# Two query tiles of a head pair as one attention step, with the late scores inside a projection half unit

## What is computed

```
qa, ka = rms_norm over each head;  qr, kr = rope(...)        # rotary on the retention queries and keys
# prompt: query chunk c (64 frames) attends to its own chunk and the 8 before it, so to all keys <= its chunk
logits = q @ k^T * 64**-0.5 + bias[head, clipped distance];  p = softmax(logits);  o = p @ v
# sample: 64 queries attend to 512 cached keys and their own 64
```

## The kernel before

| short name | on PE | what follows elsewhere |
|---|---|---|
| S | `scores(k)`, L1951; sample tile L1958 to L1960 | DVE `add_bias` (L1260), ACT `exponentials` (L759, L763), DVE `scale_probs` (L1269, L1273) |
| H | `half_unit`, L1901 | DVE rotation, then the low part of the next unit |
| P | `probs(k-1)`: transposes, L1973, L1976 | ACT `probs_out`, copies to `pt` (L744, L746) |
| V | `values(k-2)`: p times v, L1993, L1998 | ACT `attn_out` once per pair |
| C | `cache_keys`: transposes of cached keys, L1938 | ACT copies to `kc_t` (L726); the sample tile's scores need it |

## Time and profile before

### The profile page before, as it was taken

How to read it: one execution, slowest core, us unless ns; L and a number is a source line. 1 busy time by engine, 2 the same in 40 slices (tenths; PEclk the granted TensorE clock), 3 DMA queues, 4 the chain that set the end, 5 groups by cost and what they waited for, 6 DMA issues and landing times.

```text
span 1425.9 us, 29063 instructions
## 1 busy us (share of the span) xinstructions
PE 1417.3 (99%) x10910; PEld 1376.4 (97%) x10910; DVE 1002.2 (70%) x1946; ACT 623.2 (44%) x1097; POOL 46.9 (3%) x89
## 2 busy tenths in 40 slices
PE   9999999999999999999999999999999999999999
PEld 8998889999999999999999988899999999999998
DVE  7348755879998359995442777567899963799832
ACT  5223445746554125553222245456465531355421
POOL 2001100100000000000010011001000000000000
PEclk9999999999999999999999999999999999999999
DMA  8223421332333223323253253115133332333332
GB/s 243 80 66 116 130 60 49 124 103 77 101 88 110 83 74 91 102 79 102 70 148 89 60 159 93 46 53 164 54 103 94 88 102 61 95 109 92 94 92 74
DMA packets 226511, 136.22 MB, mean 96 GB/s; under 512 B 4777, under 2 KB 220513, under 8 KB 226417
## 3 DMA queue, kind: packets, MB, share of 16 engines
q1 hardware_dynamic: 220240, 113.82, 28.5%
q0 software_dynamic: 5936, 20.82, 4.6%
q10 hardware_dynamic: 240, 0.32, 0.1%
HBM read 122.04 MB, written 8.18 MB: 91 GB/s over the span
## 4 chain that ended last, share of the span: by engine, by line
PE 96%; DVE 3%; issue 1%; ACT 1%; DVEq 0%; ACTq 0%
PE ps L1753 37%; PE ps L2164 34%; PE ps L1901 13%; PE ps L1951 2%; PE ps L1993 1%; PE ps L1973 1%; PE ps L1803 1%; PE ps L2244 1%; DVE sc L1260 1%; PE ps L2044 0%; DVE lo_of L1053 0%; PE ps L1811 0%; PE ps L2053 0%; PE ps L2071 0%; PE ps L1998 0%
## 5 line engine op out<-in xcount | busy, mean ns | idle before, releaser
L1753 PE MATMUL ps<-act,hi_down 128*128 128x288 f32 x1364 | 271.9, 295 | 0.0
L1753 PE MATMUL ps<-mix,hi_of 128*128 128x288 f32 x1216 | 243.7, 296 | 1.1 <-DVE lo_of L1053 1.0
L1753 PEld LDWEIGHTS ps<-act,hi_down 128*128 128x128 f32 x1364 | 218.4, 188 | 0.0
L1901 PE MATMUL ps<-mix,hi_of 128*128 128x288 f32 x1024 | 211.3, 300 | 0.0
L1753 PE MATMUL ps<-act,lo_down 128*128 128x288 f32 x682 | 201.0, 295 | 0.0
L1753 PEld LDWEIGHTS ps<-mix,hi_of 128*128 128x128 f32 x1216 | 194.3, 188 | 2.0 <-DVE lo_of L1053 1.5
L1753 PE MATMUL ps<-mix,lo_of 128*128 128x288 f32 x608 | 179.1, 295 | 0.0
L1901 PEld LDWEIGHTS ps<-mix,hi_of 128*128 128x128 f32 x1024 | 162.6, 188 | 10.4 <-issue 8.0
L1901 PE MATMUL ps<-mix,lo_of 128*128 128x288 f32 x512 | 150.8, 295 | 0.0
L901 ACT ACTIVATE hi_S<-sum_S 128x512 fp32r<-128x512 f32 x176 | 106.5, 628 | 95.3 <-DVE sum_S L1477 93.7
L2164 PE MATMUL ps<-sums_a,hi_A 128*128 128x288 f32 x704 | 142.7, 295 | 0.2
(11 more groups left out here) (272 smaller groups left out, 2698.0 us busy)
## 6 DMA issues: line engine op xcount, KB each, us to landing
raw_of<-in_w_in SPq DMA_DIRECT2D x56, 512.0 KB, 3.8
raw_down<-in_w_down SPq DMA_DIRECT2D x32, 704.0 KB, 4.6
pair_raw<-in_w_gate SPq DMA_DIRECT2D x42, 512.0 KB, 4.0
pair_raw<-in_w_up SPq DMA_DIRECT2D x42, 512.0 KB, 5.2
raw_of<-in_w_out SPq DMA_DIRECT2D x16, 512.0 KB, 4.1
mix<-att POOLq DMA_DIRECT2D x8, 576.0 KB, 5.8
strip_even<-bias_lines POOLq DMA_DIRECT2D x8, 320.0 KB, 5.9
strip_odd<-bias_lines POOLq DMA_DIRECT2D x8, 320.0 KB, 5.5
```

The source lines that it names most:

```text
L1753: last = nc.tensor.matmul(ps[:, bank + half, 0:HALF], weights(w, slot, nk)[:, k, :], tile[:, part, HALF * half:HALF * half + HALF], start= ...
L1901: last = nc.tensor.matmul(ps[:, half_bank(i), 0:HALF], weights(w, n % 2, KD)[:, k, :], mix[:, k, part, HALF * half:HALF * half + HALF], st ...
```

## The change

Tiles 0 and 1 of a pair become one item. Its scores lie side by side in a PSUM bank (128 and 256 columns), it has one round of waits, six transposes in one P, and the value products of both tiles in one V. A layer has 16 items instead of 20, and 18 steps, each with a half unit. The sample tile's scores are issued within their step's half unit, after 18 of its 24 matmuls. In that step DVE does the rotation ahead of `add_bias`. The small tiles `least`, `sums` and `rsum` are widened from 2 to 4 columns. The rotations of the six early half units use another scratch row (`qk_masked_row`), so that the first of them waits for `qk_lo` instead of `tok_ps`; the wait on `tok_ps` now stands ahead of the attention loop. Counts of semaphores follow the number of items.

```diff
@@
         PAIRS = HA // 2
-        ITEMS_A = [(p, t) for p in range(PAIRS) for t in range(TT)]
+        TILES_A = ((0, 1), (2,), (3,), (QT,))
+        IA = len(TILES_A)
+        ITEMS_A = [(p, tiles) for p in range(PAIRS) for tiles in TILES_A]
         NA = len(ITEMS_A)
         STEPS_A = NA + 2
...
-        AT_A = [k for k in range(STEPS_A) if k % TT != QT - 1]
+        AT_A = list(range(STEPS_A))
...
+        def keys_of(tiles):
+            at = [sum(P * (u + 1) for u in tiles[0:i]) for i in range(len(tiles) + 1)]
+            return [(t, slice(at[i], at[i + 1])) for i, t in enumerate(tiles)]
@@ ScalarE
                 for k in range(STEPS_A):
-                    if k >= TT + 2 and (k - 2) % TT == 0:
-                        attn_out((k - 2) // TT - 1)
-                    if k % TT == 3 and k < NA:
-                        cache_keys(k // TT)
+                    if k >= IA + 2 and (k - 2) % IA == 0:
+                        attn_out((k - 2) // IA - 1)
+                    if k % IA == IA - 1 and k < NA:
+                        cache_keys(k // IA)
@@ VectorE, half_unit
+                        swapped = qk_masked_row if i < PRE else vt[:, 0, :]
                         nc.vector.tensor_tensor(dst, bank, rcos[:, c], ALU.mult)
-                        nc.vector.tensor_tensor(vt[0:H, 0, c], bank[H:P, :], rsin[H:P, c], ALU.mult)
...
+                        nc.vector.tensor_tensor(swapped[0:H, c], bank[H:P, :], rsin[H:P, c], ALU.mult)
...
                     if i == 0:
-                        dve.wait_ge(tok_ps, 3 * TT * l + TT)
+                        dve.wait_ge(qk_lo, l + 1)
                     half_unit(i)
@@ VectorE, the loop of the attention steps
+                dve.wait_ge(ret_ready, 16 * l + PRE)
+                dve.wait_ge(tok_ps, 3 * TT * l + TT)
                 for k in range(STEPS_A + 1):
-                    if k < NA:
+                    late = k < NA and k % IA == IA - 1
+                    if k < NA and not late:
                         add_bias(k)
                     if k - 1 in AT_A:
                         half_unit(PRE + AT_A.index(k - 1))
-                    if k % TT == 1 and k < NA:
-                        decode_queries(k // TT)
+                    if late:
+                        add_bias(k)
+                    if k % IA == 1 and k < NA:
+                        decode_queries(k // IA)
                     if k < NA:
                         scale_probs(k)
@@ TensorE
-                def half_unit(i):
+                def half_unit(i, before_last=None):
...
                     for k in range(KD):
+                        if before_last and k == KD - 2:
+                            before_last()
                         for j, (w, part) in enumerate(PASSES):
...
-                        for hh in range(2):
-                            hr = head_rows(hh)
-                            last = nc.tensor.matmul(ps[:, 2 + hh, 0:P * (t + 1)], q_rev[hr, p, tok(t)], keys[hr, 0:P * (t + 1)],
-                                                    start=True, stop=True)
+                        for t, some in keys_of(tiles):
+                            for hh in range(2):
+                                hr = head_rows(hh)
+                                last = nc.tensor.matmul(ps[:, 2 + hh, some], q_rev[hr, p, tok(t)], keys[hr, 0:P * (t + 1)],
+                                                        start=True, stop=True)
...
                 for k in range(STEPS_A):
-                    late = k % TT == QT
+                    late = k % IA == IA - 1
                     if k < NA and not late:
                         scores(k)
                     if k in AT_A:
-                        half_unit(PRE + AT_A.index(k))
-                    if k < NA and late:
-                        scores(k)
+                        half_unit(PRE + AT_A.index(k), (lambda: scores(k)) if k < NA and late else None)
...
-                    if k % TT == 2 and k < NA:
-                        cache_keys(k // TT)
+                    if k % IA == 2 and k < NA:
+                        cache_keys(k // IA)
```

More of the change, by code:

```diff
@@ L735, in probs_out @@
                 def probs_out(k):
-                    p, t = ITEMS_A[k]
+                    p, tiles = ITEMS_A[k]
                     eng.wait_ge(pt_ps, NA * l + k + 1)
@@ L755, in exponentials @@
                         eng.wait_ge(sums_inv, NA * l + k - 1)
-                    if t < QT:
-                        for hh in range(2):
-                            e = sc[:, k % 2, hh, 0:P * (t + 1)]
-                            last = nc.scalar.activation(e, e, ACT.Exp, scale=-1.0, bias=least[:, k % 2, hh:hh + 1],
-                                                        accum_out=sums[:, k % 2, hh:hh + 1])
+                    if tiles[0] < QT:
+                        for i, (t, some) in enumerate(keys_of(tiles)):
+                            for hh in range(2):
+                                e, c = sc[:, k % 2, hh, some], 2 * i + hh
+                                last = nc.scalar.activation(e, e, ACT.Exp, scale=-1.0, bias=least[:, k % 2, c:c + 1],
+                                                            accum_out=sums[:, k % 2, c:c + 1])
                     else:
@@ L1248, in add_bias @@
                     strip = strips[p % 2]
-                    for hh in range(2):
+                    for i, hh in [(i, hh) for i in range(len(tiles)) for hh in range(2)]:
+                        t, some = keys_of(tiles)[i]
                         if t < QT:
                             r, w = slice(0, P), P * (t + 1)
-                            src, bias, dst = ps[:, 2 + hh, 0:w], strip[:, hh, STRIP - w:STRIP], sc[:, k % 2, hh, 0:w]
-                            c = hh
+                            src, bias, dst = ps[:, 2 + hh, some], strip[:, hh, STRIP - w:STRIP], sc[:, k % 2, hh, some]
+                            c = 2 * i + hh
                         else:
@@ L1264, in scale_probs @@
                 def scale_probs(k):
-                    p, t = ITEMS_A[k]
-                    n = 2 if t < QT else 1
+                    p, tiles = ITEMS_A[k]
+                    n = 2 * len(tiles) if tiles[0] < QT else 1
                     dve.wait_ge(exped, NA * l + k + 1)
@@ L1270, in scale_probs @@
                     dve.wait_ge(sums_inv, NA * l + k + 1)
-                    for hh in range(n):
-                        e = sc[:, k % 2, hh, 0:P * (t + 1)] if t < QT else sc_dec[:, k % 2, 0:TOK]
-                        last = nc.vector.tensor_scalar(e, e, rsum[:, k % 2, hh:hh + 1], None, ALU.mult)
+                    for c in range(n):
+                        t, some = keys_of(tiles)[c // 2]
+                        e = sc[:, k % 2, c % 2, some] if t < QT else sc_dec[:, k % 2, 0:TOK]
+                        last = nc.vector.tensor_scalar(e, e, rsum[:, k % 2, c:c + 1], None, ALU.mult)
                     last.then_inc(p_scaled, 1)
@@ L1933, in cache_keys @@
                     if p:
[L1935 removed]
+                        pe.wait_ge(s_ps, NA * l + IA * p)
                         pe.wait_ge(ot_out, PAIRS * l + p)
@@ L1969, in probs @@
                     wait_apart(pe, *waits)
-                    if t < QT:
+                    if tiles[0] < QT:
                         for hh in range(2):
-                            for s in range(t + 1):
+                            for s in range(keys_of(tiles)[-1][1].stop // P):
                                 last = nc.tensor.transpose(ps[:, 4 + hh, P * s:P * s + P], sc[:, k % 2, hh, P * s:P * s + P], ident)
```

52 lines of the change are left out of this document (27 added, 25 removed).

## The result

The changed kernel takes 1422.88 us (median of 8 runs, 1422.09 to 1423.36), the kernel before 1427.19 us beside it (1426.74 to 1427.76). The ratio is 0.9968, with a 95% interval of 0.9958 to 0.9977. That is 4.3 us faster, where 7.7 were predicted, and 0.5 us above the range. The profiled execution took 1423.22 us, its span is 1421.4 us against 1425.9.

What follows compares the result with a forecast made beforehand. PE's own instruction stream, busy for 99% of the span, was taken as the bound. 0.82 for each of 8 pairs (6.6) and 6 x 0.21 (1.3) made 7.8, taken as 7.7: 1419.4 us, range 1417.3 to 1422.4.

Steps and rivals of the forecast that it cites:

- rival A: Merged scores on PE: second tile's weights cannot load while the first streams; 1.7 us less gain, 1421.1; chance 0.12.
- rival B: DVE later than reckoned, so PE's wait before the next pair's first scores stays; 1.3 us less gain; chance alone 0.06.
- rival C: ACT's `kc_t` copy late, PE stands still inside a half unit; 1435 at 3.2 late; 0.05 in part, 0.03 slower, shared.
- Part 7: Early rotations on DVE: the first can start some 2 us earlier; worth 0, bounds 0 and 2 x 0.55.
- rival D: Rotation ahead of the bias delays DVE beyond 1.7 room; 8 us per us beyond 2.3; 0.05 in part, 0.03 slower, shared.
- five parts: PE's priced gains per pair: scores, transposes, values, cached keys, together 0.82, and the wait before the next scores, 0.21.
- 1 scores of tiles 0 and 1: PE, per pair: both tiles' scores in one group take 0.84 instead of 1.05; gain 0.21.
- 2 six transposes together: PE, per pair: six transposes at 0.80, as measured on tile 2, instead of 1.10; gain taken as 0.28.
- 3 values of tiles 0 and 1: PE, per pair: both tiles' values in one group of 12 loads take 0.80 instead of 0.96; gain 0.16.
- 4 cached keys: PE, per pair: cached keys' transposes, now followed by a half unit of the same shape, take 0.42 for 0.59; gain 0.17.
- 5 wait before the next scores: PE: sample scores start 0.79 earlier, so the wait before the next pair's scores loses 0.21, six times, 1.3 us.
- its other bound: Six transposes on PE reckoned from 0.44 for two plus 2 x 0.11 x 2, giving 0.88 instead of 0.80.

Runs made afterwards that it cites:

- sixth experiment: The changed kernel with the cached keys' transposes between the values of tile 0 and tile 1, two more shape changes per pair: 1425.52 us.
- first experiment: The changed kernel with ACT's copy of token tile 0 between the exponentials of tiles 0 and 1 in each layer's first attention step: 1421.47 us.
- seventh experiment: The changed kernel with the cached keys' transposes between the half unit and the six transposes, no longer behind the values: 1422.99 us.

## Why the prediction was right and where it failed

The mechanism was right and the sum too large, by 3.4 us: 7.7 predicted, 4.3 measured between the medians.

**Right.** The merged scores take 0.85 (0.84 predicted), so rival A is out. By the rule of the Trainium skill (TensorE: Matmul & The Clock Gate, Part 3: Packing small matmuls) the second tile's loads, in the same row groups, would not have overlapped and the group would take 1.05; the trace shows eight loads within 0.52 and 0.85 in all, so the rule did not decide here. The prediction said that no scores before could show it, but they did: of tile 0's four loads in two halves of rows the third starts at 145.66, while the first two matmuls run and 0.1 before the next one starts at 145.76. The merged values took 0.80 as predicted, the cached keys gained 0.20 instead of 0.17, and a change of shape costs 0.17 by the sixth experiment. The wait for `least` went (rival B out). ACT ended `kc_t` at 188.54, 1.22 ahead of the sample scores at 189.76, where 1.2 was worked out (rival C out). DVE's low part was ready at 189.31, 2.0 before the sample scores' bias at 191.31, where 1.7 was worked out. That bias ended at 192.86, 0.69 before the scores at 193.55, where 0.6 was. The rows, in the third pair:

```profile
187.95 0.59 ACT L733 ACTIVATE kc_t<-ps 128x512 f32<-128x512 f32 x1
```

```profile
188.08 1.23 DVE L1061 TENSOR_TENSOR lo_of<-raw_of,hi_of 128x1024 fp32r<-128x1024 f32 x1 [1.14 <-ACT hi_of L641]
...
191.31 0.75 DVE L1270 CUSTOM_DVE_ANT_0 sc<-ps,strip_even 64x576 f32<-64x576 f32 x1 [2.01 <-PE ps L1979]
...
192.78 0.08 DVE L1270 DVE_READ_ACCUMULATOR2_ANT least<- 64x1 f32 x1
```

Part 7 was priced at 0 and is 0. The wait of the earlier trace rows is still there:

```profile
113.43 0.19 PEld L1930 LDWEIGHTS ps<-qk_part,spread_r 128*128 128x128 f32 x1 [0.55 <-DVE qk L1224]
```

**Wrong, 1.7 us: a step was missing.** The prediction asked what DVE and ACT must have ready in a middle pair and checked it well. For the first step of a layer it said only, under rival D, that ACT "also copies `vr`", and did not price it. Merging two items puts their four exponentials ahead of whatever ACT has behind the first item, and in the first step that is the copy on which PE's fifth token tile waits. Its price could have been bounded: the exponentials start 1.08 later, and the two more take 1.0 (126.01 to 126.99), less 0.3 by which ACT was idle before. Of that 1.7, 0.5 is the token transposes' own later start (125.00 for 124.52), and the copy had 0.4 of room before (it ended at 125.88, the fifth tile started at 126.29). That leaves 0.8. By the trace it is 2 x 0.84; the first experiment gave 1.62 of it back.

**Wrong, 1.3 us: terms mis-sized.** From the second pair before (24.85) to a pair of the changed kernel (24.00) the gain is 0.85, where the five parts have 0.82 + 0.21 = 1.03:

| part | predicted | measured | from the starts |
|---|---|---|---|
| 1 scores of tiles 0 and 1 | 0.21 | 0.20 | 1.05 to 0.85 |
| 2 six transposes together | 0.28 | 0.23 | 1.10 to 0.87 |
| other transposes of the pair | 0 | -0.13 | 0.80 to 0.88, 1.04 to 1.09 |
| 3 values of tiles 0 and 1 | 0.16 | 0.16 | 0.96 to 0.80 |
| 4 cached keys | 0.17 | 0.20 | 0.59 to 0.39 |
| 5 wait before the next scores | 0.21 | 0.20 | 1.01 to 0.81 |
| half units, sample scores, rest | 0 | -0.01 | |

The two lines of transposes make up the 0.18 by which this pair falls short. The prediction counted the merged group close to the price of a group behind a pause; it had 0.88, which is right to 0.01, as its other bound and took 0.28 of gain from between the two. It also overlooked that the six of tile 2, which followed scores, and the eight of tile 3, which followed sample scores, would now follow a half unit. The seventh experiment shows that it is the place and not the group that makes the difference. Over a layer the attention fell short by 3.91 - 2.43 = 1.48, of which 0.84 is the first step; the 0.64 left are 0.16 for each pair, 1.3 in all.

**Elsewhere, 0.3 us.** The two attentions gained 4.8 and the span 4.5. The first scores start 0.07 later, and in the retention of layer 0 the idle time ahead of the scores grew (L2064, 1.5 in all over both layers against 1.3 for L2044), so that the stretch between the two attentions takes 0.26 more. I did not test this.

So the 7.8 of the sum less 1.7, 1.3 and 0.3 is 4.5, against 4.5 between the two spans and 4.3 between the medians. The mechanism of all five parts held. What failed is one path that was left out, the token copy in each layer's first step, and the price of the transposes. The range counted a spread of 1.3 us for the sizes of the terms and named no one-time cost of the first step. With the first experiment's copy in place the kernel takes 1421.47, which lies within it.

## What to carry to other kernels

Where one engine is busy for 99%, read the starts of its instructions group by group: a fixed price was paid on the path here each time PE entered or left products that use halves of the array, and fewer, larger groups save it. Take the price of a group only from a row whose neighbour ahead is the same as it will be after the change, and ask of each group that stays whether its neighbour changes. When two items of a software pipeline are merged, look at everything that stood between them or behind the first of them on every engine, the one-time work of the first step above all, since a loop's middle says nothing of it. Where medians of two variants differ by more than their traces do, compare the granted clocks of the runs before looking for another cause.

## What the runs showed of the hardware

- To enter or leave the products that take turns in halves of the array (64\*128 scores, 128\*64 values) costs PE 0.17 us on its path, whatever the size of the groups around it (16 more changes cost 2.77 us in the trace). Next to the sample tile's 64\*64 loads it is 0.07. A smaller load alone costs nothing: transposes go from 128\*128 to 128\*64 with no idle time. The Trainium skill (TensorEngine Tiling (Array Packing), Key Properties) says that changing the mode drains TensorE and has no figure.
- Loads for a second query tile run ahead of streams in the same rows of the array: eight loads of 64\*128 issue within 0.52 us.
- Which instruction comes first on ACT decides where its table load stands: in an idle stretch, or 1.28 us on the path, as soon as copies are put ahead of the exponentials. The Trainium skill (ScalarE: Activation LUTs, What ACT_TABLE_LOAD costs) has 1.283 us for the load, which the trace shows, and 1.38 more for a drain. The trace shows no such pause around it: copies end at 127.00, the load starts at 127.02, the exponential at 128.31.
- The granted clock fell from 2.4 to 1.2 GHz for some 3 us right behind a wait of 2.6 us of PE's weight loads, which cost 1.5 us; the same wait in the other layer of the same execution was followed by no fall.
- A wait that the profile gives to "issue" in the weight loads can be another engine's after all: the 0.88 before the last four token transposes went when ACT's copy was moved, and the row of the matmuls had named ACT, with 0.67.
